# A rotary embedding's partner dimensions: a permutation product on TensorE, or DMA copies between SBUF tiles

## The reference, cut to what matters

```python
def apply_partial_rope(t, cos, sin):          # SWA: 16 of 64 dimensions, halves of 8
    half = ROPE_DIM // 2
    t1, t2, rest = t[..., :half], t[..., half:ROPE_DIM], t[..., ROPE_DIM:]
    return jnp.concatenate([t1 * cos - t2 * sin, t2 * cos + t1 * sin, rest], axis=-1)

def apply_rope(x, cos, sin):                  # DA and DSA: 64 of 64, halves of 32
...
    x1, x2 = jnp.split(x.astype(jnp.float32), 2, axis=-1)
    return jnp.concatenate([x1 * c - x2 * s, x2 * c + x1 * s], axis=-1).astype(x.dtype)
```

## Time and profile before

| | |
|---|---|
| median of three runs | 2853.04 us (2849.44 to 2856.81) |
| span of the profiled execution | 2846.9 us, from its first to its last instruction |
| its own time beside the span | not recorded; the median lies 6.1 us over the span |
| TensorE, share of the span with a product at work | 88% |
| ScalarE, VectorE, GpSimd busy | 35%, 53%, 29% |
| mean share of the 16 DMA engines | 21% |

### The profile page before, as it was taken

The page is one execution under the profiler, slowest core; times in us unless marked ns, Lnnn a source line. Parts: engine busy times, 40 slices in busy tenths (PEclk is TensorE's granted clock), DMA queues, the critical chain, the costliest instruction groups (busy, mean ns, idle before and its releaser), DMA issues. The chain is left out here.

```text
span 2846.9 us, 42949 instructions
## 1 busy us (share of the span) xinstructions
PE 2498.0 (88%) x15847; PEld 2128.1 (75%) x15847; DVE 1521.1 (53%) x2207; ACT 1008.5 (35%) x1900; POOL 829.1 (29%) x357
## 2 busy tenths in 40 slices
PE   6988886788997789997789989889899977999898
PEld 5777775556664578885789989877666647999897
DVE  4767766433333454444467774259644425777722
ACT  3433332333442344553333332233333323333422
POOL 1444442333220311110234443322110003355342
PEclk8999998899997889996889999978899968999998
DMA  4222211242210211110223332311110102233321
GB/s 116 74 60 66 59 37 30 60 89 60 52 28 9 61 50 44 37 44 0 60 74 88 90 94 82 75 45 31 45 28 24 37 1 75 74 88 88 90 83 49
DMA packets 344144, 163.60 MB, mean 57 GB/s; under 512 B 66991, under 2 KB 342216, under 8 KB 344056
## 3 DMA queue, kind: packets, MB, share of 16 engines
q1 hardware_dynamic: 343672, 161.83, 21.0%
q0 software_dynamic: 384, 0.58, 0.1%
HBM read 160.29 MB, written 2.10 MB: 57 GB/s over the span
## 5 line engine op out<-in xcount | busy, mean ns | idle before, releaser
L261 PE MATMUL ps<-h_parts,parts 128*128 128x264 f32 (+1 forms) x10208 | 1672.6, 314 | 113.8 <-DVE wide_parts L285 49.8
L261 PEld LDWEIGHTS ps<-h_parts,parts 128*128 128x128 f32 x10208 | 1473.7, 195 | 226.6 <-issue 56.2
L236 POOL TENSOR_TENSOR parts<-ring,parts 128x1024 fp32r<-128x1024 f32 (+1 forms) x286 | 754.5, 2640 | 1833.8 <-ACT parts L228 1831.9
L228 ACT ACTIVATE parts<-ring 128x1024 fp32r<-128x1024 f32 (+1 forms) x286 | 310.7, 1091 | 521.7 <-PE ps L261 258.1
L261 PE MATMUL ps<-wide_parts,parts 128*128 128x264 f32 (+1 forms) x1152 | 353.6, 307 | 0.0
L1883 DVE SCALAR_TENSOR_TENSOR up_c<-up_u,vec,up_c 128x528 f32<-128x528 f32 x88 | 224.5, 2551 | 11.9 <-DVE up_c L1882 0.3
L261 PEld LDWEIGHTS ps<-wide_parts,parts 128*128 128x128 f32 x1152 | 222.3, 193 | 8.0
L1857 ACT ACTIVATE up_u<-ps 128x264 f32<-128x264 f32 x176 | 68.8, 391 | 342.8 <-PE ps L261 342.8
L1357 PE MATMUL ps<-wide 64*128 64x128 f32 (+3 forms) x480 | 155.0, 427 | 20.2 <-ACT wide L1482 13.0
L1033 DVE TENSOR_TENSOR norm_acc<-norm_acc,norm_sq 128x528 f32<-128x528 f32 (+1 forms) x48 | 114.3, 2381 | 75.9 <-ACT norm_sq L1004 75.9
L863 DVE SCALAR_TENSOR_TENSOR ssm_conv<-wide,vec,ssm_conv 128x512 f32<-128x512 f32 x96 | 118.5, 1234 | 11.3 <-DVE ssm_conv L861 0.2
(11 more groups left out here) (268 smaller groups left out, 2715.4 us busy)
## 6 DMA issues: line engine op xcount, KB each, us to landing
ring<-in_ffn_w_up SPq DMA_DIRECT2D x88, 512.0 KB, 3.8
ring<-in_ssm_w_in SPq DMA_DIRECT2D x48, 512.0 KB, 3.9
ring<-in_ffn_w_down SPq DMA_DIRECT2D x32, 704.0 KB, 4.7
ring<-in_att_w_in SPq DMA_DIRECT2D x48, 256.0 KB, 3.6
ring<-in_da_w_qkv SPq DMA_DIRECT2D x24, 512.0 KB, 3.8
ring<-in_dsa_w_in SPq DMA_DIRECT2D x24, 512.0 KB, 3.8
ring<-in_ssm_w_out SPq DMA_DIRECT2D x16, 512.0 KB, 3.6
ring<-in_att_w_out SPq DMA_DIRECT2D x8, 512.0 KB, 3.8
```

The lines of the kernel that those rows point to most:

```text
L228: self.nc.scalar.activation(self.part(st, u, 0), self.slot(u, st.kt), ACT.Copy).then_inc(self.w_high, 1)
L236: self.nc.gpsimd.tensor_tensor(self.part(st, u, 1), self.slot(u, st.kt), self.part(st, u, 0).bitcast(F32), ALU.subtract).then_inc(self.w_l ...
L261: m = self.nc.tensor.matmul(out, w[:, n], b, start=start and f == j == 0, stop=stop and f == st.kt - 1 and j == 2)
```

## The change

The products with `rot1` and `rot2` in SWA, DA and DSA are taken out. Behind the eviction of a `raw` tile ScalarE waits for its own copy and issues four DMAs from `raw` to a new SBUF tile `turned` (8 partitions of 2 KB each in SWA, 32 partitions of 2.1 KB each in DA and DSA), which swap the partner dimensions. VectorE reads `turned` where it read PSUM. The sign moves from the matrix to the sine table: `sin1` gets it through a scale by a column of constants, `sin2` has it in the constants. The index stage of DSA keeps its product, with an unsigned matrix (`swap2`). The eviction of the next head's tile now waits for the four DMAs to have read `raw`, and the DMAs wait until VectorE has used `turned`. The semaphores of `project` are shared by all its calls. The core of the diff:

```diff
-        nc.scalar.activation(k.sin1[:], self.ang, ACT.Sin).then_inc(self.s_a, 1)
+        nc.scalar.activation(k.sin1[:], self.ang, ACT.Sin, scale=k.sign1).then_inc(self.s_a, 1)
...
+        t1, t2, turned = sb("t1", [P, SEQ]), sb("t2", [P, SEQ]), sb("turned", [P, 3, SEQ])
...
-                def rot(s, q):
-                    pe.wait_ge(sem["lin_free"], 6 * s + order[q] + 1)
-                    if q == 0:
-                        wait(pe, sem["pt"], 4 * s)
-                    if q == 2:
-                        pe.wait_ge(sem["rope"], 3 * s + 1)
-                    nc.tensor.matmul(ps[:, 4 + q % 2, :], k.rot1, raw[:, q, :], start=True, stop=True).then_inc(sem["rot"], 1)
...
+                        nc.scalar.activation(raw[:, j, :], src, ACT.Copy).then_inc(sem["lin_free"], 1)
+
+                        act.wait_ge(sem["lin_free"], 6 * i + q + 1)
+                        for b in (0, 8, 64, 72):
+                            o = b ^ 8
+                            act.dma_start(turned[o:o + 8, j, :], raw[b:b + 8, j, :]).then_inc(s_turned[j], 16)
...
-                        dve.wait_ge(sem["rot"], 3 * s + q + 1)
-                        do(v.tensor_tensor(t2[:], ps[:, 4 + q % 2, :], k.sin1[:], ALU.mult))
+                        dve.wait_ge(s_turned[q], 64 * s + 64)
+                        do(v.tensor_tensor(t2[:], turned[:, q, :], k.sin1[:], ALU.mult))
...
-                                pv(s - 1, 3), trans(s - 1, 4)
-                            if att:
-                                rot(s, 0)
-                            if tail:
-                                pv(s - 1, 4)
-                            if att:
-                                rot(s, 1)
-                                if diff:
-                                    vtr(s)
+                                pv(s - 1, 3), trans(s - 1, 4), pv(s - 1, 4)
+                            if att and diff:
+                                vtr(s)
...
                     if u < 2:
-                        wait(act, sem["rot"], 2 * i - 1 + u if not isinstance(i, int) or i else 0)
+                        wait(act, s_turned[u], 64 * i)
...
                     nc.scalar.activation(dst, ps[:, b, 0:HALF], ACT.Copy).then_inc(sem["lin_free"], 1)
+                    if u < 2 and b:
+
+                        act.wait_ge(sem["lin_free"], NP * i + q + 1)
+                        wait(act, sem["rope"], 2 * i - 1 + u if not isinstance(i, int) or i else 0)
+                        for j in range(0, P, 32):
+                            o = j ^ 32
+                            act.dma_start(turned[o:o + 32, u, :], raw[j:j + 32, u, :]).then_inc(s_turned[u], 16)
```

More of the change, by code:

```diff
@@ L78, in constants @@
     cos2, sin2 = np.cos(ang).astype(np.float32), np.sin(ang).astype(np.float32)
-    return np.concatenate([eye, ones, tri, rot1, rot2, before, causal, cos2, sin2, inv1], axis=1)
+    sign1 = np.where(d < 8, -1, 1).astype(np.float32)[:, None]
+    sin2 = np.where(d < 32, -1, 1).astype(np.float32)[:, None] * sin2
+    return np.concatenate([eye, ones, tri, rot2, before, causal, cos2, sin2, inv1, sign1], axis=1)
 def wait(eng, sem, value):
@@ L162, in __init__ @@
         self.loads = [0] * self.SLOTS
+        self.project_done, self.project_free, self.project_half = (self.sem("project_" + x) for x in ("done", "free", "half"))
+        self.projected = self.halved = 0
         self.acc, self.sq, self.rstd = sb("norm_acc", [P, T2]), sb("norm_sq", [P, T2]), sb("norm_rstd", [P, T2])
@@ L1051, in swa @@
         sem = {x: k.sem("swa_" + x) for x in (
-            "lin_done", "lin_free", "rot", "rope", "vtr", "v", "s", "nm", "exp", "es", "pn", "t", "pt", "pv", "out")}
+            "lin_done", "lin_free", "rope", "vtr", "v", "s", "nm", "exp", "es", "pn", "t", "pt", "pv", "out", "clear")}
+        s_turned = [k.sem(f"swa_turned{q}") for q in range(3)]
         steps = Steps(k.sem("swa_steps"))
@@ L1249, in step @@
                     steps.end()
+                v.memset(turned[:], 0.0).then_inc(sem["clear"], 1)
                 pre.dve(dve)
@@ L1278, in pairs @@
         rop, t1, t2 = k.wide[:, 10:12, :], k.wide[:, 12:14, :], k.wide[:, 14, :]
+        turned = sb("turned", [P, 2, T2])
         vT, vt = k.wide[:, 15, :], sb("v", [P, 5, P])
@@ L1289, in pairs @@
         sem = {x: k.sem(f"{name}_{x}") for x in (
-            "lin_done", "lin_free", "cos", "rot", "rope", "v", "s", "nm", "exp", "pn", "t", "pt", "pv", "o") + (
+            "lin_done", "lin_free", "cos", "rope", "v", "s", "nm", "exp", "pn", "t", "pt", "pv", "o") + (
             ("vtr", "osq", "oss", "rstd", "out") if diff else ())}
+        s_turned = [k.sem(f"{name}_turned{q}") for q in range(2)]
         steps = Steps(k.sem(name + "_steps"))
@@ L1324, in piece @@
                         m.then_inc(sem["lin_done"], 1)
-                def rot(s, q):
-                    if q == 0:
-                        pe.wait_ge(sem["lin_free"], NP * s + NP)
-                        wait(pe, sem["exp"], 10 * s)
-                    elif not diff:
-                        wait(pe, sem["o"], 5 * s)
-                    for b in range(2):
-                        m = nc.tensor.matmul(ps[:, 4 - 2 * q + b, 0:HALF], k.rot2, raw[:, q, b * HALF:(b + 1) * HALF], start=True, stop=True)
-                    m.then_inc(sem["rot"], 1)
                 def vtr(s):
+                    pe.wait_ge(sem["lin_free"], NP * s + NP)
                     wait(pe, sem["o"], 5 * s)
@@ L1346, in scores @@
                     if n == 0:
+                        wait(pe, sem["exp"], 10 * s)
                         pe.wait_ge(sem["rope"], 2 * s + 2)
@@ L1579, in step @@
                     for q in range(2):
-                        dve.wait_ge(sem["rot"], 2 * s + q + 1)
-                        do(v.tensor_tensor(both(t2), ps[:, 4 - 2 * q:6 - 2 * q, 0:HALF], both(k.sin2), ALU.mult))
+                        dve.wait_ge(s_turned[q], 64 * s + 64)
+                        do(v.tensor_tensor(t2, turned[:, q, :], k.sin2, ALU.mult))
                         v.tensor_tensor(rop[:, q, :], t1[:, q, :], t2, ALU.add).then_inc(sem["rope"], 1)
```

42 lines of the change are left out of this document (19 added, 23 removed).

## The result

The changed kernel takes 2858.84 us (median of 15 runs, 2855.13 to 2861.37), the kernel before 2850.2 us in 15 runs beside it. The ratio is 1.0031, 95% interval 1.0023 to 1.0039: slower by 0.3%, where 2826 us was forecast. Some runs of the third group of experiments and of the kernel before beside it, at 3550 to 4808 us, were in a slower state; every median and ratio here is of the others.

A forecast was written before the change was run, and what follows sets the result against it. TensorE, busy 88% of the span, was taken as the bound. Removal -34.1, issues +6.0 and clock +1.5 gave -26.6 us, from a median of 2853.0 to 2826 us; range 2814 to 2845.

The forecast's parts named there:

- The transfers are hidden: DMA copies in SWA, DA and DSA, priced at nothing; the tightest, DSA's key tile, has 9 us.
- DSA's last head: Removing the rotations in DSA's last head, at half clock, gives 4.0 us.
- DSA's removal: Removing DSA's rotation products gives 1.9 us for each of six steady heads, 11.4 us; 15.4 us with the last head.
- The hold of `nm` by GpSimd's subtraction: DA and DSA: a subtraction under way holds VectorE's `nm` until its end; if nothing held it, 2818 us.
- What is added: issues on ScalarE: Four DMA issues per tile at 0.37 us each, hidden in SWA, costing +6.0 us in DA and DSA together.
- In the key tile's slot it loses 0.1 us: DSA, per head: the key tile's slot loses 0.1 us to the issues; both DSA slots together -2.4 us over seven heads.
- The bounds of 0 and 0.94: Range in us for one ScalarE issue, 0.37 taken; at 0.94 the result is 2865 us.
- Issues eat the gain: Rival: issues at 0.65 to 0.8 us, or removed products were cover elsewhere; 2846 to 2860 us, chance 0.12.
- DA's first rotation: In DA's steady heads it covers a ScalarE wait, so removal gives nothing; the second rotation gives 1.0 us a head.
- SWA's last step: TensorE has some 4 us less to do there, so more may run at low clock: +1.5 us, bounds 0 and 4.
- a falling clock in the attention stages: One of three signs that the prediction is wrong: the clock of the attention stages falls.
- DA's issues: DA: the later subtraction holds `nm` until 5.45 us after the eviction; 1.0 plus 0.2 us a head, +8.4 us over seven.

The follow-up runs named there:

- third group of experiments: Follow-ups were timed beside the kernel before in three groups on one chip each; the kernel before took 2849.23, 2848.81 and 2849.71 us.
- the wait filled by useful work: Changed kernel with ScalarE's issues behind the high part in DA and DSA, and tiles of the next piece moved into TensorE's two waits: 2814.38 us.
- the two windows: DSA in the changed kernel, and in the changed kernel with only DSA's key tile issues moved behind the high part: 2839.87 us, ratio 0.9965.
- the early piece: Against the kernel with SyncE issuing DA's and DSA's copies: tiles of the next piece moved ahead of value products that wait; 2814.84 us.
- the kernel with all copies on SyncE: Kernel with SyncE issuing DA's and DSA's copies and next-piece tiles moved into TensorE's waits, SWA's copies now issued by SyncE too: 2813.14 us.

## Why the prediction was wrong

The stretches, forecast by the prediction's own terms and measured in the span (us):

| | forecast | measured |
|---|---|---|
| ahead of SWA | 0 | -5.7 |
| SWA | -6.2 | -2.0 |
| DA, first to eighth head | +0.4 | +12.3 |
| from there to DSA's first head | -3.0 | -1.6 |
| DSA, first to eighth head | -13.8 | +11.3 |
| behind it | -4.0 | -4.2 |
| sum | -26.6 | +10.1 |

**Right.** The transfers are hidden but for the first heads. DSA's last head came as forecast, -4.2 us for -4.0. The rotation in DA covers a wait of ScalarE, which then showed at 1.06 us. DSA's removal was sized well: 11.4 us for the steady heads, 10.9 measured with the copies left out. In SWA the issues are hidden. The hold of `nm` by GpSimd's subtraction is real: it came and went with the subtraction's place in every run. The Trainium skill, page "SBUF — State Buffer", section "SBUF: two separate sides", says of the ports that GpSimd and some of VectorE's operations share that whichever starts first keeps them; the 2.31 us of an `nm` that started 0.07 us too late agree.

**The step that failed most** is "What is added: issues on ScalarE", and in it the sentence "In the key tile's slot it loses 0.1 us". With 0.37 us an issue the subtraction would end some 5.45 us after the eviction, 0.1 us past the point where `nm` is ready (5.35). With 0.61 us it ends at 6.44. That `nm` is the head's last and stands on the chain to the value products. This one place cost 20.4 us in DSA where 0.7 was priced. The 0.37 us (the row's least; its median is 0.38) was that of another kind of DMA, a weight load; SyncE needs 0.59 us for these copies. The bounds of 0 and 0.94 held the true value, but the sum was drawn as a line between them (gain used up "at about 0.75 us an issue"), and the cost is no line. At 0.61 us that line gives some 2843 us; the kernel took 2858.84 and was already slower than before. The time lies in the range of the rival "Issues eat the gain", 2846 to 2860 us, at a lower price than its 0.65 to 0.8 us.

**The second** is the clock. The prediction counted "nothing" for DA's first rotation, since the wait ends at the same moment with or without it, and allowed the clock 1.5 us in SWA's last step only, though it named a falling clock in the attention stages as a sign of being wrong. In fact the uncovered wait is followed by 3.4 to 6.8 us at half clock in every steady head. The removal in DA, a gain of 6 us in steady heads by the prediction, became a loss of 3.2 over the seven periods, with no copy made. With the wait filled by useful work, DA is at 267.0 us, 10.8 below before: the time was there, and was given back as clock. In DSA most of the 20.4 us is clock too. Between the two windows TensorE's idle time differs by 6.6 us, which is seven waits longer by 0.96; the other 13.8 us are busy time of the same products, at a clock of 0.87 in place of 0.93.

**A term right in size by another way.** DA's issues were priced at 8.4 us, by `nm` held until 5.45 us after the eviction. Measured between ahead of and behind the high part: 9.0 us. But `nm` is 0.17 us everywhere in the changed kernel's DA; the issues pushed the subtraction past it. What is late are ScalarE's exponentials, 0.44 us in the slot read above, and TensorE's clock is lower again (0.93 and 0.95). By the windows 3.1 of the 9.0 us are idle time of TensorE, the other 5.9 busy time of the same 1787 products at the lower clock. By heads 3.0 of them fall in the first (49.17 and 46.17 us), where VectorE waits 2.8 us for a copy in the one kernel and not in the other. That the size came out is luck: the mechanism was another.

**Open.** In DSA the early piece shortens TensorE's wait (1.30 to 0.21 us) but the stretch stays at 262 us, at clock 0.85 in place of 0.91: a half-clock stretch of 10.2 us stands in every steady head, with fewer waits than before. The same DSA code took 258.4 us at 0.88 in the kernel with all copies on SyncE. So in DSA it isn't shown which wait brings the lower clock, and less waiting did not raise it. SWA's stretch took 365 us in some and 368 to 370 in other executions of the same SWA code, at the same idle time of TensorE and clocks of 0.86 and 0.85 or 0.84, so its few us of gain can't be read from one profile. The part ahead of SWA, without a rotation in any kernel, took 650.8 to 657.9 us in the profiles, so the -5.7 us there can't be put down to the change.

## What to carry to other kernels

Take the price of an issue from a DMA of the same kind, not from the same engine. Issues on a compute engine's queue are then priced by what stands behind them, not by their sum: write them behind the instruction that feeds another engine, and look up where that engine's operation then falls on a third. When removed work had covered a wait, the wait itself may cost nothing and still cost the clock behind it; move useful work into the place in the same edit, and look at the granted clock of that stretch, since in DA this gave 14 us and in DSA nothing. And a cost that arises by two operations overlapping is worked out at each bound of the unknown price, not interpolated.

## What was unexpected of the hardware

- An issue's time goes by the kind of DMA: a copy of 32 rows between SBUF tiles takes 0.61 us on ScalarE's queue and 0.59 on SyncE's, where SyncE's weight loads take 0.37. With 64 rows in place of 32 two take 1.12 us, so the rows hardly count.
- Issues of ScalarE run beside its own activation: four of 2.44 us started 0.13 us into a high part of 1.05 us, and neither grew.
- Eight microseconds of DA came back for a pair of useless products of 1.16 us a head, at a granted clock of 0.98 in place of 0.95.
